# Six of ten rotary projection tiles moved in between the groups of the third mixer's attention

## What is computed

```
def swa_sink_attention(x, pos, k_sh, v_sh, w_q, b_q, sinks, w_o, b_o):
    q = partial_rope((x @ w_q + b_q).reshape(B, S, A_Q_HEADS, A_HEAD_DIM), pos)
    ...   # blocks of 128 queries against 256 keys, masked to a band of 128
    scores = einsum(q, k) * 64 ** -0.5
    m = max(max(scores), sink);  e = exp(scores - m)
    probs = e / (sum(e) + exp(sink - m))
    return einsum(probs, v) @ w_o + b_o

def partial_rope(t, pos):          # on 16 of the 64 columns of each head; k as well
    rot = [t1 * cos - t2 * sin, t2 * cos + t1 * sin]     # t1, t2: halves of the 16
```

## Time and profile before

| | |
|---|---|
| three timed runs | 1484.62, 1484.74, 1486.32 us; median 1484.74 |
| span of the profiled execution | 1484.1 us, mean granted clock 0.999 |
| PE busy | 1475.0 us, 99% |
| weight loads (PEld) busy | 1199.4 us |
| POOL, DVE, ACT busy | 902.7, 708.6, 435.8 us |
| rotary tiles on PE | from 902.6 to 957.2 us |
| `scores(0)` to the end of `v3` | 957.2 to 971.85 us |
| groups 0 to 15 with the last spread | 971.85 to 1028.97 us |

### The profile page before, as it was taken

The page is one execution under the profiler, slowest core; times in us unless marked ns, Lnnn a source line. Parts: engine busy times, 40 slices in busy tenths (PEclk is TensorE's granted clock), DMA queues, the critical chain, the costliest instruction groups (busy, mean ns, idle before and its releaser), DMA issues.

```text
span 1484.1 us, 19739 instructions
## 1 busy us (share of the span) xinstructions
PE 1475.0 (99%) x7150; PEld 1199.4 (81%) x7150; DVE 708.6 (48%) x863; ACT 435.8 (29%) x884; POOL 902.7 (61%) x719
## 2 busy tenths in 40 slices
PE   9999999999999999999999999999999999999999
PEld 7888677888888888888888888867888888888887
DVE  5674658350046676003541284877777300552253
ACT  3242665141123422001210053766152100221032
POOL 7766035486633597666776656810659666777653
PEclk9999999999999999999999999999999999999999
DMA  6323011233311233332333322400323333233322
GB/s 208 110 89 101 22 44 57 85 100 99 99 58 56 86 108 105 99 99 89 96 99 99 99 71 86 128 30 15 100 72 113 100 99 98 89 97 99 99 85 86
DMA packets 37315, 132.72 MB, mean 89 GB/s; under 512 B 4304, under 2 KB 4736, under 8 KB 37248
## 3 DMA queue, kind: packets, MB, share of 16 engines
q1 hardware_dynamic: 36576, 129.52, 28.2%
q10 hardware_dynamic: 672, 2.23, 0.4%
HBM read 129.59 MB, written 2.10 MB: 89 GB/s over the span
## 4 chain that ended last, share of the span: by engine, by line
PE 97%; ACT 2%; DVE 1%; DMA 0%; issue 0%; SPq 0%; ACTq 0%
PE PS L644 22%; PE PS L645 22%; PE PS L646 22%; PE PS L595 3%; PE PS L596 3%; PE PS L577 3%; PE PS L826 2%; PE PS L669 1%; PE PS L670 1%; PE PS L671 1%; PE PS L1105 1%; PE PS L918 1%; PE PS L933 1%; PE PS L790 1%; PE PS L788 1%; PE PS L789 1%
## 5 line engine op out<-in xcount | busy, mean ns | idle before, releaser
L536 POOL TENSOR_TENSOR W_lo<-W_raw,W_hi 128x1024 fp32r<-128x1024 f32 x238 | 600.5, 2523 | 19.9
L533 POOL TENSOR_TENSOR HOLD<-HOLD 1x1 f32<-1x1 f32 x238 | 63.5, 267 | 544.9 <-PE PS L646 302.4
L644 PE MATMUL PS<-A_hi,W_hi 128*128 128x512 f32 x904 | 352.3, 390 | 0.1
L646 PE MATMUL PS<-A_lo,W_hi 128*128 128x512 f32 x904 | 351.8, 389 | 0.0
L645 PE MATMUL PS<-A_hi,W_lo 128*128 128x512 f32 x904 | 351.7, 389 | 0.0
L534 POOL TENSOR_SCALAR W_hi<-W_raw 128x1024 fp32r<-128x1024 f32 x238 | 247.4, 1040 | 0.0
L644 PEld LDWEIGHTS PS<-A_hi,W_hi 128*128 128x128 f32 x904 | 169.7, 188 | 36.9 <-issue 0.8
L644 PE MATMUL PS<-H_hi,W_hi 128*128 128x512 f32 x512 | 199.2, 389 | 0.0
L645 PE MATMUL PS<-H_hi,W_lo 128*128 128x512 f32 x512 | 199.2, 389 | 0.0
L646 PE MATMUL PS<-H_lo,W_hi 128*128 128x512 f32 x512 | 199.2, 389 | 0.0
L646 PEld LDWEIGHTS PS<-A_lo,W_hi 128*128 128x128 f32 x904 | 169.7, 188 | 35.3
(11 more groups left out here) (346 smaller groups left out, 2045.7 us busy)
## 6 DMA issues: line engine op xcount, KB each, us to landing
W_raw<-in_weights SPq DMA_DIRECT2D x238, 512.0 KB, 3.5
X<-in_x SPq DMA_DIRECT2D x4, 512.0 KB, 7.3
out<-X SPq DMA_DIRECT2D x7, 256.0 KB, 4.2
RELU<-in_ple_in ACTq DMA_DIRECT2D x2, 512.0 KB, 3.6
CONST<-in_constants ACTq DMA_DIRECT2D x1, 849.5 KB, 6.5
PARAM<-in_params SPq DMA_DIRECT2D x1, 320.5 KB, 8.8
SIN<-in_positions ACTq DMA_DIRECT2D x1, 256.0 KB, 3.8
out<-X SPq DMA_DIRECT2D x2, 128.0 KB, 1.7
```

The lines of the kernel that those rows point to most:

```text
L533: pool.tensor_tensor(HOLD[:, 1 + s:2 + s], HOLD[:, 0:1], HOLD[:, 0:1], ALU.add)
L536: pool.tensor_tensor(W_lo[:, s, :], W_raw[:, r, :], W_hi[:, s, :].bitcast(F32), ALU.subtract).then_inc(w_lo, 1)
L644: pe.matmul(PS[:, bank, :], W_hi[:, slot, w], hi[:, kk, :], start=first, stop=False)
L646: done = pe.matmul(PS[:, bank, :], W_hi[:, slot, w], lo[:, kk, :], start=False, stop=last)
```

## The change

The rotary tiles are multiplied in the order 0, 2, 3, 4, 5, 1, 6, 7, 8, 9. The first four stay in front (`rope3` now has four tiles); the other six become a phase `rope3b` behind `v3` in the stream. Their products are cut into units of one k (three matmuls) and put between the transposes of groups 0 to 10, in bank 0. ACT takes each with one activation; the halves are exchanged by four DMAs of 32 rows on SP's queue, which now fetches some weight blocks behind them. DVE does the rotary step in SBUF. The scores of a group come ahead of its weighing; the spread of a pair moves half a group and more later, into odd groups and bank 7, which the second transposes of these groups use too. Six of the eight k of `out3`'s first tile are multiplied in groups 11, 12, 13 and 15.

```diff
+ROPE_TILES = (0, 2, 3, 4, 5, 1, 6, 7, 8, 9)
+ROPE_FIRST = 4
+ROPED_FOR_PAIR = (2, 3, 4, 5, 7, 8, 9, 10)
...
-PHASES += [("rope3", 10, 1, "act"), ("v3", 2, 1, "dve"), ("out3", 8, 1, "dve")]
+PHASES += [("rope3", 4, 1, "act"), ("v3", 2, 1, "dve"), ("rope3b", 6, 1, "act"), ("out3", 8, 1, "dve")]
...
+FILLED_IN = (1, 2, 4, 6, 8, 10)
+OUT3_EARLY = {11: (0, 1), 12: (2, 3), 13: (4,), 15: (5,)}
+
+def filling(g):
+    for n, last in enumerate(FILLED_IN):
+        first = FILLED_IN[n - 1] + 1 if n else 0
+        if first <= g <= last:
+            each = KD // (last - first + 1)
+            return [(n, k) for k in range((g - first) * each, (g - first + 1) * each)]
+    return []
...
-            return 6 if S is SWA and p == SWA.pairs - 1 else SPREAD_BANK
+            return 6 if p == SWA.pairs - 1 else 7
...
+            def swap_halves(n):
+                sp.wait_ge(by_act, PLAN["rope3b"].act_before + n + 1)
+                if n >= 2:
+                    sp.wait_ge(roped, ROPE_FIRST + n - 1)
+                for to in range(0, P, ROPE_APART):
...
+                    sp.dma_start(SQ[rows, n % 2, :], raw_rope(n)[swapped, :]).then_inc(halves_swapped[n % 2], 16)
+            ahead = PLAN["rope3b"].first + W_SLOTS + RAW_SLOTS
+            fetches(RAW_SLOTS, ahead)
+            for n in range(PLAN["rope3b"].tiles):
+                swap_halves(n)
+                fetch(ahead + n, (ahead + n) % RAW_SLOTS)
+            fetches(ahead + PLAN["rope3b"].tiles, N_BLOCKS)
...
@@ PE, scores of the window attention
                     if g == 0:
                         pe.wait_ge(window_set, 1)
-                        pe.wait_ge(roped, 3)
-                        pe.wait_ge(by_act, PLAN["rope3"].before + 8)
+                        pe.wait_ge(roped, ROPED_FOR_PAIR[0])
+                        pe.wait_ge(by_act, PLAN["rope3"].before + ROPE_FIRST)
                     elif g == 1:
-                        pe.wait_ge(roped, 10)
+                        pe.wait_ge(roped, ROPE_FIRST)
                     else:
                         pe.wait_ge(SWA.exped, 4 * (g - 1))
+                        if c == 0 and ROPED_FOR_PAIR[p] > ROPE_FIRST:
+                            pe.wait_ge(roped, ROPED_FOR_PAIR[p])
...
@@ PE, the groups
                 for g in range(2 * SWA.pairs):
+                    units = filling(g)
                     transposes(2 * g)
-                    if g == 0:
-                        scores(2)
+                    if g % 2 and g > 1:
+                        spread_inverse(SWA, g // 2 - 1)
+                    fill(units[:len(units) // 2])
+                    if g % 2 and g > 1:
+                        pe.wait_ge(SWA.shared, g // 2)
                     transposes(2 * g + 1)
+                    fill(units[len(units) // 2:])
+                    begin_out3(OUT3_EARLY.get(g, ()))
+                    if g < 2 * SWA.pairs - 2:
+                        scores(g + 2)
                     if g:
                         weigh(2 * g - 2)
                         weigh(2 * g - 1)
-                        if g % 2 == 0:
-                            spread_inverse(SWA, g // 2 - 1)
-                    if 0 < g < 2 * SWA.pairs - 2:
-                        scores(g + 2)
...
@@ ACT, window attention
+                def take_rope(n):
+                    ph = PLAN["rope3b"]
+                    act.wait_ge(block_done, ph.first + n + 1)
...
+                    act.activation(raw_rope(n), PS[:, FILL_BANK, :], ACT.Identity,
+                                   bias=param("b_rope", ROPE_TILES[ROPE_FIRST + n])).then_inc(by_act, 1)
...
                     exponent(2 * g, 1)
+                    if g - 1 in FILLED_IN:
+                        take_rope(FILLED_IN.index(g - 1))
                     exponent(2 * g + 1, 0)
...
@@ DVE, window attention
+                def rope_filled(n):
...
+                    own(dve.scalar_tensor_tensor(out=QK3[:, tile, :], in0=raw_rope(n), scalar=s, in1=COS[:], op0=ALU.mult,
+                                                 op1=ALU.mult))
+                    dve.wait_ge(halves_swapped[n % 2], 64 * (n // 2 + 1))
+                    own(dve.scalar_tensor_tensor(out=SQ[:, n % 2, :], in0=SQ[:, n % 2, :], scalar=s, in1=SIN[:], op0=ALU.mult,
+                                                 op1=ALU.mult))
+                    own.wait()
+                    dve.tensor_tensor(QK3[:, tile, :], QK3[:, tile, :], SQ[:, n % 2, :], ALU.add).then_inc(roped, 1)
...
                         low_part(p - 2, stage_at, MIX[:, 0, :])
+                    if g - 2 in FILLED_IN:
+                        rope_filled(FILLED_IN.index(g - 2))
```

More of the change, by code:

```diff
@@ L348, in build @@
         HALVES, HALF_BANKS = (slice(0, 2 * P), slice(2 * P, T)), (3, 5)
+        halves_swapped = [sem(f"halves_swapped{n}") for n in range(2)]
         rope_swapped, roped, window_set = sem("rope_swapped"), sem("roped"), sem("window_set")
@@ L553, in product @@
             def product(phase, hi, lo, ready, ready_at, beside=None, woven=False,
-                        between=None, by_halves=False, apart=False, order=range(KD)):
+                        between=None, by_halves=False, apart=False, order=range(KD), begun=0):
                 ph = PLAN[phase]
@@ L639, in tile @@
                             at = b * KD + count
+                            if early(i, 1) and count < begun:
+                                continue
                             if early(i, 1):
@@ L813, in spread_inverse @@
                 pe.wait_ge(S.widened, p + 1)
+                if S is SWA and p < SWA.pairs - 1:
+                    pe.wait_ge(SWA.read_by_dve, 2 * p + 3)
                 if S is FOX and p == 0:
@@ L1150, in layer_stats, with from_a @@
                 project(l, half, 3, 1)
-            def from_a(phase, stage, beside=None, woven=False, between=None, by_halves=False, apart=False, order=range(KD)):
+            def from_a(phase, stage, beside=None, woven=False, between=None, by_halves=False, apart=False, order=range(KD),
+                       begun=0):
                 product(phase, A_hi, A_lo, a_lo, KD * A_STAGE[stage], beside=beside, woven=woven,
-                        between=between, by_halves=by_halves, apart=apart, order=order)
+                        between=between, by_halves=by_halves, apart=apart, order=order, begun=begun)
             def from_embedded(phase, beside=None, woven=False):
@@ L1222, in _ @@
             window_attention()
-            from_a("out3", "mixed3")
+            from_a("out3", "mixed3", begun=sum(len(tiles) for tiles in OUT3_EARLY.values()))
             layer_stats(2)
@@ L2312, in rope @@
                 ph = PLAN["rope3"]
-                for i in range(10):
-                    s = 1.0 if i < 2 else QK_SCALE
+                for i in range(ROPE_FIRST):
+                    tile = ROPE_TILES[i]
+                    s = 1.0 if tile < 2 else QK_SCALE
                     dve.wait_ge(rope_swapped, i + 1)
@@ L2320, in rope @@
                     dve.wait_ge(by_act, ph.before + i + 1)
-                    own(dve.scalar_tensor_tensor(out=QK3[:, i, :], in0=RAWQ[:, i % 2, :], scalar=s, in1=COS[:],
+                    own(dve.scalar_tensor_tensor(out=QK3[:, tile, :], in0=RAWQ[:, i % 2, :], scalar=s, in1=COS[:],
                                                  op0=ALU.mult, op1=ALU.mult))
                     own.wait()
-                    dve.tensor_tensor(QK3[:, i, :], QK3[:, i, :], PS[:, 4 + i % 2, :], ALU.add).then_inc(roped, 1)
+                    dve.tensor_tensor(QK3[:, tile, :], QK3[:, tile, :], PS[:, 4 + i % 2, :], ALU.add).then_inc(roped, 1)
             def copy_constants():
```

63 lines of the change are left out of this document (56 added, 7 removed).

## The result

The changed kernel takes **1499.7 us**, median of four runs (1497.5 to 1501.4), against 1485.5 for the kernel before in the same comparison: ratio 1.0097, 95% interval 1.0083 to 1.0112. It is slower by 14.2 us; the forecast was 1496.6 us, from a sum of +11.9. The profiled execution spans 1497.4 us, 13.3 more than the 1484.1 of before. The kernel before takes 1484.6 to 1484.8 us in most runs and about 1.7 more in the others, and of its four runs here two are of the longer kind, by its span the profiled one among them (1484.1, timed 1486.32), so that against its usual 1484.7 the change costs 15.0 us.

The account below looks back on a forecast made before the run. PE's list of work was taken as the bound (busy 1475.0 of 1484.1 us). +8.0 +1.7 -6.0 +8.2 gave +11.9, so 1496.0, with 0.6 from span to median 1496.6 us; range 1488.5 to 1503.

Parts of the forecast that it names:

- Part 1: Ahead of scores(0): PE stands until ACT has read the first four rotary tiles, +8.0 us.
- Part 2: Behind that pause: the granted clock falls to half, +1.7 us, bounds nothing and twice that.
- Part 3: scores(0), v3 and scores(1): take 14.65 us as before, nothing to add.
- Part 4: Attention groups without waits: fewer array changes and covered gaps, -4.4 us to group 10, -1.65 after; -6.0 together.
- Part 5: Waits in the groups and at out3's first tile: +8.2 us together, bounds 0 and about 11.
- Shared bank: Second transposes of groups 11, 13, 15: PE waits 0.96 us each for shared, +2.9 us.
- Last k of `out3`: out3's first tile: its k = 7 waits for the last low part, +2.4 us.
- Last groups: Last transposes: with the spread in between and no scores left to cover, +1.2 us.
- Group 4: Ahead of group 4: DVE's rotary step in group 3 delays the next maxima, +1.7 us.
- Part 6: ACT's copies, SP's DMAs and DVE's rotary steps in SBUF cost nothing, as long as POOL's splits miss them.
- Rival C: Much slower: rotary steps meet POOL or wait for exchanged halves, +17 to +25, 1501 to 1510 us; chance 0.10.
- Rival B: Faster: units absorb all of PE's small gaps, -12.6 us, giving 1480; chance 0.06.

Follow-up runs that it names:

- e1: The changed kernel with the first half of the values' product ahead of scores(0) and scores(1) behind the second half; 1489.7 us, ratio 1.0032.
- e2: The changed kernel with all of the values' product ahead of both scores and two units ahead of the first transposes; 1488.3 us, ratio 1.0024.
- e3: The changed kernel with 33 extra matmuls that nobody reads put on PE in the pause ahead of scores(0); 1495.4 us, ratio 1.0071.
- e4: The kernel before with only the scores of group g+2 moved ahead of the weighing, spread unmoved, no units filled in; 1492.5 us, ratio 1.0049.
- e8: The kernel before, ten rotary tiles in front, with the changed kernel's group order and spread in bank 7, no units; 1495.9 us, ratio 1.0075.
- e11: e4 with the next maxima ahead of DVE's product in odd groups and ACT's high-part copy behind three of four exponentials; 1482.3 us, ratio 0.9981.
- e6: e2 with five units of out3's third tile put between the last spread and the first tile's k = 6 and 7; 1485.9 us, ratio 1.0009.
- e5: e2 with out3's six early units moved between the spread and the wait for shared in groups 11, 13, 15; 1487.8 us, ratio 1.0023.

## Why the prediction was right, and where it was not

**Part 1, the pause: right**, 8.09 for 8.0 us (7.8 more than the 0.26 that stood there before), its releaser the copy of the fourth tile, as named. The rates it was made of held as well: ACT's 2.62 and 0.69 us a tile are the same in the profile after. e1 and e2 show that it is the cover, since the pause goes with it.

**Part 2, the clock: right in kind, too small.** 2.65 us for 1.7. The row it was sized by the earlier trace rows followed a pause of 1.85 us and lasted 3.4; here the clock was still at 0.50 six microseconds after the restart. The measured loss lies between the row's size and the bound of twice it. The second slow stretch, 1.6 us behind the 2.64 us wait, was in no term of the sum though the wait was in it: a wait of 2.4 us, longer than the one of the earlier trace rows, should have got a clock term too. The sentence on the Trainium skill ("TensorE: Matmul & The Clock Gate", "HAM oscillation") agrees with the trace behind the 8.09 us pause. At the 2.64 us wait the profiles go both ways: half clock behind it in three, full clock in e1 and e3. Without its clock term the sum would have missed the 2.65 us at `scores(0)` altogether.

**Part 3: nothing to add** beyond the clock; with it at 1.00 the stretch was 14.6 us (e3).

**Part 4, the gaps: wrong as an argument, and about half in size.** With the wait of Part 5 groups 0 to 10 were forecast at -2.7 and measured at -2.0, but that nearness is luck: the wait was put 1.1 us too high, and without waits the stretch gained 2.6 us where the term says 4.4. I had expected a pair with eight units at 12.2 us; it is 12.47. Of the 1.57 us of gaps 1.25 remain (7.03 less 5.78), so 0.32 were saved where I had 0.63. A part of these 1.25 is no gap: between the transposes the units' weight loads start 0.233 us apart (962.53 to 964.86, ten steps), not 0.227, which is 0.13 a pair. But the step itself, that the order has three changes of array for four and so saves time, failed: with nothing else changed the order costs 7.9 us (e4) or 11.1 (e8). I had counted PE's gaps for the new order, and not walked DVE's and ACT's queues through it. With both queues reordered (e11) a pair is 6.88 us, close to the 6.72 I had written: the price of the gaps was right, the condition for it was missing.

**Part 5, the waits.** Shared bank: right, 1.02 us each for 0.96, three of them. Last k of `out3`: right, 2.64 for 2.4; e6 gets nearly all of it back. Last groups: wrong, 0.49 and 0.45 ahead of the transposes, but 0.46 and 0.49 stood there before as well, so nothing was added where I had 1.2. Timelines of weight loads, the last transposes before (the first two rows) and after:

```profile
1025.13 0.42 PEld L933 LDWEIGHTS PS<-CONST,PR 128*128 128x128 f32 x4 [0.46 <-ACT PR L1406]
1026.04 0.42 PEld L933 LDWEIGHTS PS<-CONST,PR 128*128 128x128 f32 x4 [0.49 <-ACT PR L1406]
...
1035.10 0.42 PEld L990 LDWEIGHTS PS<-CONST,PR 128*128 128x128 f32 x4 [0.49 <-ACT PR L1504]
...
1036.99 0.42 PEld L990 LDWEIGHTS PS<-CONST,PR 128*128 128x128 f32 x4 [0.45 <-ACT PR L1504]
```

Group 4: too large, 0.64 over the usual 0.17 for 1.7. The rotary step's three operations take 0.68 to 0.69 us each, where I allowed up to 0.90, and from maxima to transposes it is 2.8 us (972.12 to 974.91), not 3.3. The stretch from group 11 came out at +4.9, as summed, again by luck: its waits are 3.06 and 2.64 us, so the gaps gave 0.8 where I had 1.65, and the 1.2 that did not come made up for it. What the part lacked is what e5 shows: the waits are one chain, so that their sum is what they cost, and not what covering one of them gives.

**Part 6: right in its result.** DVE's rotary operations in SBUF never met POOL. One reading behind it was wrong: the 0.90 us of the earlier trace rows was not beside an idle POOL, which was splitting until 922.63 (L536, 2.40 us from 920.23); free of POOL the same operation takes 0.68 to 0.69. All 18 are alike; two of the three forms, all six tiles, in the view of tile SQ of the changed kernel (least, median and largest ns, first and last start), and the exchange by DMA below them:

```profile
L2099 DVE SCALAR_TENSOR_TENSOR SQ<-SQ,SIN x6: 684/685/687, 970.8 to 1024.1; 128x512 f32<-128x512 f32 x6
L2102 DVE TENSOR_TENSOR QK<-QK,SQ x6: 691/692/693, 971.5 to 1024.8; 128x512 f32<-128x512 f32 x6
...
DMA to landing us min/median/max: 1.9/2.0/2.8
```

No instruction waited for an exchanged half. Rival C falls with this; the 31 us of DVE work that were its price did not come. Rival B (gaps that vanish, 1480) named its condition as 1.0 of 1.57 us a pair; 0.32 were absorbed.

Taken together the sum was 1.4 us under the profile's difference. Missing were 0.9 and 1.6 us of clock and 0.7 in the groups, the pause was 0.2 too high, and the start of the kernel, by luck, gave 1.7 back. Against 15.0 like for like the sum is 3.1 short. The last step, that a run lies 0.6 us above the span, was wrong as well: a run lies 2.2 above its own span (1499.6 and 1497.4; 1486.32 and 1484.1), and the span of 1484.1 belongs to the run of 1486.32, not to the median. The two errors nearly cancel, so the 1496.6 is what 11.9 on the usual 1484.7 gives. The mechanisms that carried the forecast, pause and waits, were the right ones. What I would not have found from it is why the change could not pay: the gain it was to bring lay in the queues of DVE and ACT.

## What to carry to other kernels

Moving scores ahead of the weighing gives nothing until the engines that read them can take them: walk each in-order queue through the new order, and put an instruction that waits for a late result (here DVE's product, then ACT's copy) behind those whose inputs are ready. Before work is moved to fill waits, look at what it covered where it stood: six tiles that hid ACT's 3.35 us a tile left 8 us of pause and a slow clock. And when a wait is covered, look whether it returns at the next instruction (e5) or is gone (e6): only one at the end of its chain is worth its own length.

## What the runs showed of the hardware

- The granted clock behind a pause is not a fixed price. After 8.09 us without a matmul it was at 0.50 for about 6 us of work; after waits of 2.63 to 2.64 us at the last k of `out3` it fell to 0.50 in the profiles of the changed kernel, e2 and e5, for about 3 us, and stayed at 1.00 in those of e1 and e3; after the 2.12 us of e1 it stayed at 1.00. What decides is open.
- Matmuls on data that nobody reads held the clock at 1.00 through the pause (e3), and were worth 2.65 us there.
- In the whole attention, with transposes, half-array matmuls and gaps of 0.17 to 0.42 us between the weight loads, the clock stayed at 1.00 (33.38 us of before; in e11 29.00 us from 982 to 1011, PE busy in all of them).
- A change of the array's shape costs PE about 0.17 us: in e11 a pair has six of them and takes 1.10 us more than its work (6.88 less 5.78). It is paid not only between full-array and half-array work but also between scores (64x128) and weighing (128x64): from 983.31 to 984.37 in e11 1.06 us pass for 0.86 us of scores. No order here removed it.
- A DVE operation with both inputs in SBUF took 0.68 to 0.69 us with POOL idle (18 of 18 in the changed kernel), and 2.65 beside POOL's splitting.
